# Second-table gathers of 32 slots for four tokens, mixed in TensorE's four column groups

## The chip, the cores and the metric
The kernel runs on one core of one Trainium2 chip. The metric is the device time of one execution in microseconds, lower is better.

## The reference
One inference step of a two-layer trunk for 512 prompt tokens and 8 sample tokens, in float32 with a model width of 1024. Each layer has a mixer (retention in layer 0, an S5 state space in layer 1) and a PEER expert mixer. The change lies in PEER:

```python
def peer_block(xb, w_q, key1, key2, u_tab, v_tab):
    q = (xb @ w_q).reshape(T, PEER_HEADS, 2, PEER_DQ // 2)          # 8 heads
    s1 = einsum('thd,hkd->thk', q[:, :, 0], key1)                    # 128 keys a side
    s2 = einsum('thd,hkd->thk', q[:, :, 1], key2)
    v1, i1 = top_k(s1, 16);  v2, i2 = top_k(s2, 16)
    cand = (v1[..., :, None] + v2[..., None, :]).reshape(T, PEER_HEADS, 256)
    cidx = (i1[..., :, None] * 128 + i2[..., None, :]).reshape(T, PEER_HEADS, 256)
    top, sel = top_k(cand, 16)
    eidx = take_along_axis(cidx, sel, axis=-1)                       # 8 x 16 = 128 experts a token
    gate = softmax(top, axis=-1)
    act = gelu(einsum('thkd,td->thk', take(u_tab, eidx), xb))
    return einsum('thk,thkd->td', gate * act, take(v_tab, eidx))
```

Both tables have 16384 rows of 1024 numbers (4 KB) per layer. For each token 128 rows of `u_tab` are multiplied with the token's vector, and 128 rows of `v_tab` are summed with the weights that result.

## The kernel before
The prompt is four tiles of 128 tokens, one token to a partition; the samples are a fifth tile of 8 rows. A token's 128 experts are its slots. A chunk is 32 slots (two heads) of one tile (`CH`), four chunks make a tile (`PARTS`), 16 a layer (`CHUNKS`).

Pool (GpSimd) issues every table gather by an indirect DMA: row p of the gather is the table row that token p's index names, so one gather brings one slot of 128 tokens, 128 rows of 4 KB. Rows of the first table (u) land in `v_ring` during the first two chunks and in `u_ring` after that, rows of the second (v) in `v_ring`; each has 8 places (`RING`). The order is written out by hand in Pool's `peer`: the first two chunks are u alone, then a u gather of chunk j alternates with a v gather of chunk j-2 (`LAG`). After the last u come v gathers alone, from `LATE` on (the last 16 slots) with the 8 sample gathers ahead of them. A gather waits until its place is free: u places by `u_used` (DVE), v places by `v_used` (PE) or `v_added` (DVE).

DVE multiplies each u row with the token's vector and sums it (L2346). Between these products stand pieces of the selection of the next chunk (`best_of`), the softmax, and the weights of the chunk before. For a v slot ACT writes a 128x128 diagonal of the slot's weights (`diagonal`, L1620), and PE multiplies the diagonal with the 128 gathered rows (`mix`, L1982; two matmuls, which the profile shows as four records), summing in two PSUM banks per tile. Eight diagonals exist (`DIAGS`); ACT waits for PE before it writes one again. 19 slots near the end of a layer (`DVE_SLOTS`) are summed by DVE instead (L2389). The selection of a chunk begins with scores on PE (L1929) and their copy by ACT (`scores_in`, L1591), which stands in ACT's program behind the diagonal of slot 14 of a chunk and waits for `top_done`, a finished selection that frees the buffer. In chunks 7, 9, 11 and 12 two scores are computed, one of them for the samples.

At the end of a layer `sample_mix` (L1967) multiplies the sample rows, and DVE adds each tile's sum to the residual (`mixed`, L2311 and L2315), the last tile's when its last slot is summed; the norm for the next part follows.

## Time and profile before

| | |
|---|---|
| median of 3 runs | 4188.11 us (4186.7 to 4188.8) |
| profiled execution, span from its first to its last instruction | 4188.0 us, mean granted TensorE clock 0.952 |
| PE busy | 3358.3 us (80%) |
| DVE busy | 2484.9 us (59%) |
| Pool busy | 2098.5 us (50%) |
| ACT busy | 690.1 us (16%) |
| DMA | 1293.90 MB, mean 309 GB/s |

Shares of busy time are means over the retention, SSM and PEER parts, which have different limits; a stage is read by its own windows and by what ended the waits in it. In a timeline row the first number is the start, the second the duration, and the bracket is how long the engine was idle just before and who ended that.

### The profile page before, as it was taken

The page shows a single profiled execution, that of the slowest core. Times are in us where ns is not written, and L with a number is a line of the kernel's source. Part 1 is how long each engine was busy: PE and PEld are TensorE (multiplying, and loading weights), DVE is VectorE, ACT ScalarE, POOL GpSimd, SP SyncE. Part 2 cuts the span into 40 slices and gives each one's busy share as a digit, 9 for nine tenths or more (in the row PEclk, how much of TensorE's full clock was granted, in tenths as well). Part 3 has the DMA queues.
Part 4 walks back from the last instruction along what each step waited for, and adds up shares of the span by engine and source line. Part 5 has one row for each costly group of instructions (what it writes and reads, how often), then busy time and mean ns, then how long its engine had stood idle before and what let it go on. Part 6 is the DMA issues. An engine that isn't in the chain of part 4 may idle for free.

```text
span 4188.0 us, 31521 instructions
## 1 busy us (share of the span) xinstructions
PE 3358.3 (80%) x9470; PEld 1378.2 (33%) x9470; DVE 2484.9 (59%) x5918; ACT 690.1 (16%) x1670; POOL 2098.5 (50%) x2213
## 2 busy tenths in 40 slices
PE   6899999996777777777778847996777787768777
PEld 1343443463222222222222334452222232223222
DVE  4334334449666776778652483259667676877643
ACT  2211111111111111111111232101111111111111
POOL 1110010016777767777775010026777677767766
PEclk8799999998999999999999968998999999989999
DMA  9943243249999999999999344159999999999998
GB/s 333 312 151 121 96 145 116 95 143 338 409 409 409 409 392 404 409 402 394 406 409 392 109 44 142 46 185 367 409 409 409 409 394 406 409 399 396 409 409 309
DMA packets 409876, 1293.90 MB, mean 309 GB/s; under 512 B 50094, under 2 KB 73806, under 8 KB 408687
## 3 DMA queue, kind: packets, MB, share of 16 engines
q0 software_dynamic: 309312, 1126.31, 68.6%
q1 hardware_dynamic: 100232, 163.58, 12.3%
q10 hardware_dynamic: 180, 2.18, 0.2%
q8 instruction: 71, 1.16, 0.1%
q14 instruction: 81, 0.66, 0.0%
HBM read 1263.06 MB, written 28.85 MB: 308 GB/s over the span
## 4 chain that ended last, share of the span: by engine, by line
PE 30%; DMA 26%; POOL 20%; DVE 13%; issue 8%; ACT 2%; SPq 1%; DVEq 0%; POOLq 0%; ACTq 0%
DMA arena<-in_peer_v_dram,arena 13%; DMA w<-in_peer_u_dram,arena 11%; POOL arena L1362 10%; POOL w L1362 9%; PE ps L1802 8%; PE ps L1982 5%; DVE arena L2346 3%; PE ps L1894 3%; DVE w L2346 3%; PE ps L809 3%; PE ps L1949 3%; DMA w<-in_w_ada_dram 2%; PE ps L701 1%; PE ps L1760 1%; PE ps L1735 1%
## 5 line engine op out<-in xcount | busy, mean ns | idle before, releaser
L1982 PE MATMUL ps<-arena 128*128 128x512 f32 x3944 | 1946.0, 623 | 642.7 <-DMA arena<-in_peer_v_dram,arena 553.4
L2346 DVE CUSTOM_DVE_ANT_0 w<-w,ps 128x1024 f32<-128x1024 f32 x896 | 1090.1, 1218 | 695.8 <-DMA w<-in_peer_u_dram,arena 694.1
L1982 PEld LDWEIGHTS ps<-arena 128*128 128x128 f32 x3944 | 691.9, 192 | 1872.1 <-DMA arena<-in_peer_v_dram,arena 1220.7
L1362 POOL DMA_INDIRECT arena<-in_peer_v_dram,arena x1040 | 1000.9, 962 | 431.4 <-issue 239.7
L1362 POOL DMA_INDIRECT w<-in_peer_u_dram,arena x912 | 860.6, 944 | 280.8 <-issue 249.4
L1620 ACT ACTIVATE arena<-ident,arena 128x128 f32<-128x128 f32 x986 | 377.2, 398 | 1611.9 <-PE ps L1982 1587.1
L1802 PE MATMUL ps<-w,hT 128*128 128x512 f32 x768 | 341.7, 598 | 0.0
L1949 PE MATMUL ps<-hT,w 128*128 128x512 f32 (+1 forms) x512 | 262.2, 605 | 0.0
L1362 POOL DMA_INDIRECT arena<-in_peer_u_dram,arena x128 | 124.6, 974 | 217.3 <-DVE arena L2346 143.6
L1802 PEld LDWEIGHTS ps<-w,hT 128*128 128x128 f32 x768 | 142.7, 190 | 195.7 <-issue 175.4
L1303 POOL TENSOR_TENSOR rstd<-var,mhalf 128x1 f32<-128x1 f32 x25 | 16.5, 666 | 287.9 <-DVE var L2015 287.9
L2346 DVE CUSTOM_DVE_ANT_0 arena<-arena,ps 128x1024 f32<-128x1024 f32 x128 | 151.8, 1214 | 9.7 <-DMA arena<-in_peer_u_dram,arena 9.7
L1334 POOL DMA_DIRECT2D out_dram<-arena x16 | 11.6, 726 | 281.3 <-DVE arena L2118 276.6
L1894 PE MATMUL ps<-w,arena 128*128 128x512 f32 (+1 forms) x320 | 142.0, 598 | 0.0
L1950 PEld LDWEIGHTS ps<-hT,w 128*128 128x128 f32 x512 | 97.3, 190 | 108.7 <-issue 91.8
L2389 DVE SCALAR_TENSOR_TENSOR arena<-arena 128x1024 f32<-128x1024 f32 x36 | 46.3, 1287 | 114.4 <-DMA arena<-in_peer_v_dram,arena 114.2
L2194 DVE MAX8 arena<-modp 128x8 f32<-128x128 f32 (+1 forms) x160 | 34.6, 277 | 102.4 <-ACT modp L1591 102.4
L1529 ACT ACTIVATE arena<-ps 128x512 f32<-128x512 f32 (+1 forms) x60 | 35.7, 595 | 349.8 <-PE ps L1802 345.2
L1342 POOL TENSOR_TENSOR rstd<-var,mhalf 128x1 f32<-128x1 f32 x20 | 12.8, 640 | 154.5 <-DVE var L2099 154.5
L535 POOL MEMSET arena<- 64x2048 f32 x4 | 10.7, 2672 | 157.1 <-DVEq L1041 157.0
L1296 POOL TENSOR_TENSOR mods<-arena 9x1024 f32<-9x1024 f32 x4 | 11.2, 2799 | 150.2 <-ACT arena L1482 150.2
L2346 DVE DVE_READ_ACCUMULATOR2_ANT arena<- 128x1 f32 x1024 | 84.2, 82 | 0.0
(319 smaller groups left out, 2962.6 us busy)
## 6 DMA issues: line engine op xcount, KB each, us to landing
w<-in_w_ada_dram SPq DMA_DIRECT2D x32, 1024.0 KB, 11.7
w<-in_ret_w_in_dram SPq DMA_DIRECT2D x24, 1024.0 KB, 7.3
arena<-in_peer_v_dram,arena POOLq DMA_INDIRECT x1040, 10.3
x<-in_w_ada_dram SPq DMA_DIRECT2D x16, 1024.0 KB, 11.6
w<-in_peer_w_q_dram SPq DMA_DIRECT2D x16, 1024.0 KB, 8.0
w<-in_peer_u_dram,arena POOLq DMA_INDIRECT x912, 10.8
out_dram<-arena POOLq DMA_DIRECT2D x20, 512.0 KB, 5.0
arena<-in_state_ret_dram POOLq DMA_DIRECT2D x16, 512.0 KB, 6.0
```

The source lines that it names most:

```text
L701: mm = pe.matmul(ps[:, t % 2, :], hT[:, c, t * P:(t + 1) * P], block_rows(b)[:, c, :], start=(c == 0), stop=(c == KC - 1))
L809: mm = pe.matmul(ps[:, 2 * (n % 2) + b, :], hT[:, c, t * P:(t + 1) * P], rows_of[b][:, c, :], start=(c == 0), stop=(c == KC - 1))
L1362: pool.indirect_dma_start(ring[:, slot, :], None, table, bass.IndirectOffsetOnAxis(ap=index, axis=0)).then_inc(landed_sem[slot], 16)
L1620: act.activation(diag[:, n % DIAGS], ident[:, :], ACT.Copy, scale=wgt[:, m % 4, s:s + 1]).then_inc(diag_done, 1)
L1735: mm = pe.matmul(ps[32 * j:32 * j + 32, 1 + n % 2, :], condT[:, c, :], ada_rows[slot][:, c, :], start=(c < 4), stop=(c >= 4))
L1802: mm = pe.matmul(ps[:, bank, :], hT[:, c, t * P:(t + 1) * P], block_rows(j % 2)[:, c, :], start=(c == 0), stop=(c == KC - 1))
L1894: mm = pe.matmul(ps[0:rows, n % 4, :], oT[:, c, t * P:t * P + rows], rows_out[:, c, half * BW:(half + 1) * BW], start=(c == 0), stop=(c == 3))
L1949: pe.matmul(ps[:, n % 2, first:TP * P], wq, hT[:, c, first:TP * P], start=(c == 0), stop=(c == KC - 1))
L1950: mm = pe.matmul(ps[:, 2 + n % 2, 0:NS], wq, hT[:, c, TP * P:NTOK], start=(c == 0), stop=(c == KC - 1))
L1982: mm = pe.matmul(ps[:, bank + half, :], diag[:, n % DIAGS], v_ring[:, n % RING, half * BW:(half + 1) * BW], start=(n % NE == 0), stop=(n % ...
L2346: dve.tensor_tensor_reduce(row, row, h_ps, 1.0, 0.0, ALU.mult, ALU.add, acts[:, j % 2, s:s + 1]).then_inc(u_used, 1)
L2389: dve.scalar_tensor_tensor(v_sum, v_ring[:, n % RING], weight, v_sum, ALU.mult, ALU.add)\
```

## The change
A v gather no longer brings one slot of 128 tokens, but the chunk's 32 slots of four tokens: partition 32q+s holds slot s of token 32j+8q+r, for q = 0 to 3. A chunk has 32 such gathers, numbered 4r+j. The index table for it, `eidx_t`, is made by PE, which turns a chunk's places (`turn_places`: four matmuls against strided columns of the identity), and DVE, which copies them out of PSUM (`places_out`). Four gathers (j = 0 to 3) make a batch. In it column group j of PE (32 columns, so 32 PSUM partitions) multiplies gather j with 32 columns of a zeroed strip (`windows`) in which four columns hold the turned weights, so that each of the four tokens gets the sum over its 32 slots. The strip's place slides with r. The weights are turned by PE (`turn_weights`) and copied into the strip by ACT (`windows_of`), once per chunk and not once per slot. The diagonals and the slots summed by DVE are gone. A batch is 8 matmuls of 32x512 (16 records); its four places come free together. Three semaphores are new (`turned_ps`/`turned_done`, `windows_ps`/`windows_done`, and PE's waits on `score_done` ahead of the turns, which use the scores' banks). `gated`, the product in `mixed`, moves to other memory, and DVE clears `windows` once per layer.

```diff
-DIAGS = 8
+GROUPS = 4
+TURNS_IN = CH // GROUPS
+WINDOWS = TURNS_IN * (NE + 1)
...
-DVE_SLOTS = ([CH * (CHUNKS - 2) + s for s in range(11, CH, 3)] + [CH * (CHUNKS - 1) + s for s in range(2, 15, 3)] +
-             [LATE + s for s in range(0, 13, 2)])
...
+        by_group = ident.rearrange("p (j q r) -> p q r j", j=GROUPS, q=GROUPS)
...
+        turned_places = ps[:, 4, 0:2 * CH]
+        turned_weights = ps[:, 5, 0:CH]
...
                 def v_gather(n):
                     place = v_place(n)
                     if n < RING:
                         pool.wait_ge(u_used, used_before(layer, SWITCH - RING + n + 1))
                     else:
-                        v_free(place - RING)
-                    gather(v_ring, place % RING, vt, eidx[:, n // NE, n % NE:n % NE + 1], v_ld)
+                        pool.wait_ge(v_used, used_before(layer, place - RING + 1))
+                    if n % CH == 0:
+                        pool.wait_ge(turned_done, CHUNKS * layer + n // CH + 1)
+                    gather(v_ring, place % RING, vt, eidx_t[:, n // CH, n % CH:n % CH + 1], v_ld)
...
-                def diagonal(m, s):
-
-                    n = TP * NE * layer + CH * m + s
-                    if CH * m + s in DVE_SLOTS:
-                        return
-                    if s == 0:
-                        act.wait_ge(wgt_done, (CHUNKS + 1) * layer + m + 1)
-                    if CH * m + s >= DIAGS:
-                        act.wait_ge(v_used, mixed_before(layer, v_place(CH * m + s - DIAGS) + 1))
-                    act.activation(diag[:, n % DIAGS], ident[:, :], ACT.Copy, scale=wgt[:, m % 4, s:s + 1]).then_inc(diag_done, 1)
+                def windows_of(m):
+
+                    act.wait_ge(windows_ps, CHUNKS * layer + m + 1)
+                    if m >= 2:
+                        act.wait_ge(v_used, used_before(layer, v_place(CH * (m - 1) - 1) + 1))
+                    rows_of = windows[:, m % 2].rearrange("p (r n) -> p r n", n=NE + 1)
+                    for q in range(GROUPS):
+                        part_ = slice(CH * q, CH * (q + 1))
+                        at = TURNS_IN * q
+                        ins = act.activation(rows_of[part_, :, at:at + 3 * CH + 1:CH],
+                                             turned_weights[part_].rearrange("p (r j) -> p r j", j=GROUPS), ACT.Copy)
+                    ins.then_inc(windows_done, 1)
...
+                windows_of(0)
+                for j in range(LAG, CHUNKS + 1):
+                    tanh_of(j - 1)
+                    if j == CHUNKS:
+                        for i in range(TP - 1):
+                            squares(k, i)
+                        tanh_of(CHUNKS)
+                    if j + 1 < CHUNKS:
+                        for p in TOPS[j + 1]:
+                            scores_in(p)
+                    if j < CHUNKS:
+                        for p in TOPS[j]:
+                            exponentials(p)
+                    windows_of(j - 1)
...
+                def turn(out, source):
+
+                    for q in range(GROUPS):
+                        mm = pe.matmul(out[CH * q:CH * (q + 1)], source, by_group[:, q], start=True, stop=True)
+                    return mm
+
+                def turn_places(m):
+
+                    pe.wait_ge(top_done, picked_at(layer, PLACE[m // PARTS, m % PARTS]))
+                    if m >= 2:
+                        pe.wait_ge(turned_done, CHUNKS * layer + m)
+                    at = CH if m == 1 else 0
+                    turn(turned_places[:, at:at + CH], place[:, m % 3]).then_inc(turned_ps, 1)
+
+                def turn_weights(m):
+
+                    pe.wait_ge(wgt_done, (CHUNKS + 1) * layer + m + 1)
+                    if m:
+                        pe.wait_ge(windows_done, CHUNKS * layer + m)
+                    turn(turned_weights, wgt[:, m % 4]).then_inc(windows_ps, 1)
+
+                def mix(m, r):
+
+                    t, bank = m // PARTS, 2 * (m // PARTS % 2)
+                    if m % PARTS == 0 and r == 0 and t >= 2:
                         pe.wait_ge(mix_free, TILES * layer + t - 1)
-                    pe.wait_ge(v_ld[n % RING], landed(layer, v_place(n)))
-                    pe.wait_ge(diag_done, diagonals_before(layer, n + 1))
+                    if r == 0:
+                        pe.wait_ge(windows_done, CHUNKS * layer + m + 1)
+                    n = CH * m + GROUPS * r
+                    for j in range(GROUPS):
+                        pe.wait_ge(v_ld[(n + j) % RING], landed(layer, v_place(n + j)))
                     for half in range(2):
-                        mm = pe.matmul(ps[:, bank + half, :], diag[:, n % DIAGS],
-                                       v_ring[:, n % RING, half * BW:(half + 1) * BW],
-                                       start=(n % NE == 0), stop=(n % NE == NE - 1))
-                    mm.then_inc(v_used, 1)
-
+                        for j in range(GROUPS):
+                            at = NE * r + CH * j
+                            mm = pe.matmul(ps[CH * j:CH * (j + 1), bank + half, :], windows[:, m % 2, at:at + CH],
+                                           v_ring[:, (n + j) % RING, half * BW:(half + 1) * BW],
+                                           start=(m % PARTS == 0 and r == 0),
+                                           stop=(m % PARTS == PARTS - 1 and r == TURNS_IN - 1))
+                            if half:
+                                mm.then_inc(v_used, 1)
+
+                pe.wait_ge(score_done, picked_at(layer, TOPS[1][-1]))
+                turn_places(0)
+                turn_places(1)
+                pe.wait_ge(score_done, picked_at(layer, TOPS[2][-1]))
+                turn_weights(0)
                 for j in range(LAG, CHUNKS + LAG):
                     tops = TOPS[j + 1] if j + 1 < CHUNKS else []
-                    for s in range(CH):
-                        if CH * (j - LAG) + s == LATE:
+                    if j < CHUNKS:
+                        if TOPS[j]:
+                            pe.wait_ge(score_done, picked_at(layer, TOPS[j][-1]))
+                        turn_places(j)
+                    for r in range(TURNS_IN):
+                        if CH * (j - LAG) + GROUPS * r == LATE:
                             sample_mix()
-                        mix(j - LAG, s)
-                        if s == 8 and tops:
+                        mix(j - LAG, r)
+                        if r == 2 and tops:
+                            pe.wait_ge(turned_done, CHUNKS * layer + j + 1)
                             scores(tops[0])
-                        if s == 12 and len(tops) > 1:
+                        if r == 3 and len(tops) > 1:
                             scores(tops[1])
-                        if s == 8 and j == CHUNKS - 1:
+                        if r == 2 and j == CHUNKS - 1:
 
                             pe.wait_ge(score_done, TURNS * (layer + 1))
                             pe.wait_ge(gate_done, layer + 1)
+                            pe.wait_ge(turned_done, CHUNKS * (layer + 1))
                             pe.transpose(ps[:, 4, 0:NS], place_s[0:NS], ident[0:NS, 0:NS])
                             pe.transpose(ps[:, 4, NS:2 * NS], gate[0:NS, TP], ident[0:NS, 0:NS]).then_inc(es_ps, 1)
+                        if r == TURNS_IN - 2 and j <= CHUNKS:
+                            if tops:
+                                pe.wait_ge(score_done, picked_at(layer, tops[-1]))
+                            turn_weights(j - 1)
...
+                def places_out(m, n):
+                    dve.wait_ge(turned_ps, CHUNKS * layer + m + n)
+                    dve.tensor_copy(eidx_t[:, m:m + n].rearrange("p m n -> p (m n)"), turned_places[:, 0:n * CH])\
+                       .then_inc(turned_done, n)
...
+                        if s == 28 and j == LAG - 1:
+                            places_out(0, 2)
+                        if s == 4 and j >= LAG:
+                            places_out(j, 1)
...
-                for i, n in enumerate(DVE_SLOTS):
-                    if n == CH * (CHUNKS - 1) + 11:
-                        weights_out((CHUNKS + 1) * (layer + 1), acts_s, acts_s2, gate_s, wgt_s[:, ::NS + 1])
-                    weight = wgt[:, n // CH % 4, n % CH:n % CH + 1]
-                    dve.wait_ge(v_ld[n % RING], landed(layer, v_place(n)))
-                    if i == 0:
-                        dve.tensor_scalar(v_sum, v_ring[:, n % RING], weight, None, ALU.mult).then_inc(v_added, 1)
-                    else:
-                        dve.scalar_tensor_tensor(v_sum, v_ring[:, n % RING], weight, v_sum, ALU.mult, ALU.add)\
-                           .then_inc(v_added, 1)
-                    if n == CH * (CHUNKS - 1) + 14:
-                        for i in range(TP - 1):
-                            variance(k, i)
-                    if n >= LATE + 2 and n <= LATE + 6:
-                        normalized(k, (n - LATE - 2) // 2)
-                    dve.wait_ge(v_added, added(layer, n))
-                link.link(dve.tensor_tensor(v_sum, v_sum, modp[:, 2], ALU.mult))
-                dve.wait_ge(v_used, mixed_before(layer, LATE + NS))
+                weights_out((CHUNKS + 1) * (layer + 1), acts_s, acts_s2, gate_s, wgt_s[:, ::NS + 1])
+                for i in range(TP - 1):
+                    variance(k, i)
+                for i in range(TP - 1):
+                    normalized(k, i)
```


PE's program at the first chunks that are mixed, in the kernel before (L1929 scores, L1982 mix):

```order
L1929 MATMUL ps<-arena 128x128 x2
L1982 MATMUL ps<-arena 128x512 x18
L1929 MATMUL ps<-arena 128x128 x4
L1982 MATMUL ps<-arena 128x512 x64
L1929 MATMUL ps<-arena 128x128 x4
L1982 MATMUL ps<-arena 128x512 x64
```

The same place after the change (L1921 scores, L1966 turns, L1997 mix):

```order
L1921 MATMUL ps<-arena 128x128 x2
L1966 MATMUL ps<-ident,arena 32x32 x16
L1997 MATMUL ps<-arena 32x512 x24
L1921 MATMUL ps<-arena 128x128 x4
L1997 MATMUL ps<-arena 32x512 x32
L1966 MATMUL ps<-ident,arena 32x32 x4
L1997 MATMUL ps<-arena 32x512 x8
L1966 MATMUL ps<-ident,arena 32x32 x4
L1997 MATMUL ps<-arena 32x512 x24
```

The scores moved from behind slot 8 to behind the third batch (slots 8 to 11); the turned weights of the next chunk stand behind the seventh batch, and the turned places of a chunk ahead of the first batch of the chunk two before it.

ACT's program around chunk 7 before, with the semaphores that each waits for (L1591 copies of scores, L1620 diagonals, L1609 tanh, L1597 exponentials):

```order
L1620 ACTIVATE arena<-ident,arena 128x128 [waits v_used,wgt_done]
L1620 ACTIVATE arena<-ident,arena 128x128 [waits v_used] x4
L1609 ACTIVATE arena<-arena 128x32 [waits gelu_in]
L1620 ACTIVATE arena<-ident,arena 128x128 [waits v_used] x10
L1591 ACTIVATE modp<-ps 128x512 [waits top_done,score_ps]
L1591 ACTIVATE modp<-ps 8x512 [waits top_done,score_ps]
L1620 ACTIVATE arena<-ident,arena 128x128 [waits v_used] x12
L1597 ACTIVATE arena<-arena 128x32 [waits e_sub]
```

After (L1581 copies of scores, L1599 tanh, L1587 exponentials, L1610 the copies into the strip):

```order
L1599 ACTIVATE arena<-arena 128x32 [waits gelu_in]
L1581 ACTIVATE modp<-ps 128x512 [waits top_done,score_ps]
L1581 ACTIVATE modp<-ps 8x512 [waits top_done,score_ps]
L1587 ACTIVATE arena<-arena 128x32 [waits e_sub]
L1610 ACTIVATE arena<-ps 32x8x4 [waits v_used,windows_ps]
L1610 ACTIVATE arena<-ps 32x8x4 x3
```

Behind the two score copies, which still wait for `top_done`, no work for the running chunk is left; the copies into the strip belong to the next one.

Pool's program where the first v gather of a layer stands, after the change (before, this gather waits for `u_used` alone):

```order
L1357 DMA arena<-in_peer_u_dram,arena 128x1024 [waits u_used] x31
L1357 DMA w<-in_peer_u_dram,arena 128x1024 [waits u_used,q_ps,top_done]
L1357 DMA arena<-in_peer_v_dram,arena 128x1024 [waits turned_done,u_used]
L1357 DMA w<-in_peer_u_dram,arena 128x1024 [waits u_used]
L1357 DMA arena<-in_peer_v_dram,arena 128x1024 [waits u_used]
```

The gather itself stands where it stood; a wait for DVE's copy of the turned places is new in front of it.

## Rows read from the trace of the kernel before

**Rows 1.** The page: two rows of the 40 slices, a fortieth of the span each.

```profile
DMA  9943243249999999999999344159999999999998
GB/s 333 312 151 121 96 145 116 95 143 338 409 409 409 409 392 404 409 402 394 406 409 392 109 44 142 46 185 367 409 409 409 409 394 406 409 399 396 409 409 309
```

**Rows 2.** The page's costliest groups: busy and mean, then idle before and its end.

```profile
L1982 PE MATMUL ps<-arena 128*128 128x512 f32 x3944 | 1946.0, 623 | 642.7 <-DMA arena<-in_peer_v_dram,arena 553.4
...
L1620 ACT ACTIVATE arena<-ident,arena 128x128 f32<-128x128 f32 x986 | 377.2, 398 | 1611.9 <-PE ps L1982 1587.1
```

**Rows 3.** The timeline in the mixed stretch: an issue, and a slot's mix.

```profile
2001.43 0.94 POOL L1362 DMA_INDIRECT w<-in_peer_u_dram,arena  x1 [0.30 <-issue]
...
2003.20 1.98 PE L1982 MATMUL ps<-arena 128*128 128x512 f32 x4 [0.58 <-DMA arena<-in_peer_v_dram,arena]
```

**Rows 4.** Windows: stretch, length, busy times, PEclk, DMA share, GB/s.

```profile
1100.00:1400.00 300.00, 231.92 (x496) 82.04 (x494) 202.60 (x518) 48.74 (x128) 226.27 (x240) 1.00 1.03 409
1440.00:1940.00 500.00, 383.59 (x850) 146.55 (x848) 370.35 (x1023) 80.68 (x220) 355.41 (x376) 0.95 1.01 400
3300.00:3800.00 500.00, 381.93 (x850) 145.38 (x848) 370.39 (x1023) 80.50 (x221) 355.54 (x377) 0.96 1.01 401
```

**Rows 5.** The timeline around one dent of layer 0.

```profile
1488.93 0.59 ACT L1591 ACTIVATE modp<-ps 8x512 f32<-8x512 f32 x1 [23.59 <-DVE arena L2278]
...
1489.96 7.40 PE L1982 MATMUL ps<-arena 128*128 128x512 f32 x12 [9.84 <-ACT arena L1620]
...
1493.98 0.94 POOL L1362 DMA_INDIRECT arena<-in_peer_v_dram,arena  x1 [11.42 <-PE ps L1982]
```

**Rows 6.** The waits: total, times, longest.

```profile
PE ps L1982 <- ACT arena L1620: 85.1, 8, 13.1
```

**Rows 7.** The timeline at the first v gather of layer 0.

```profile
1020.21 0.93 POOL L1362 DMA_INDIRECT arena<-in_peer_v_dram,arena  x1 [0.30 <-issue]
...
1021.51 1.22 DVE L2346 CUSTOM_DVE_ANT_0 arena<-arena,ps 128x1024 f32<-128x1024 f32 x1
...
1026.42 0.21 DVE L2298 TENSOR_SCALAR arena<-arena 128x32 f32<-128x32 f32 x1
...
1026.77 1.22 DVE L2346 CUSTOM_DVE_ANT_0 w<-w,ps 128x1024 f32<-128x1024 f32 x1
```

**Rows 8.** PE's timeline near the start: two groups of 16 records with 32 columns.

```profile
11.14 3.64 PE L1735 MATMUL ps<-w,arena 128*32 128x512 f32 x16 [2.53 <-DMA w<-in_w_ada_dram]
...
113.73 1.92 PE L1735 MATMUL ps<-w,arena 128*32 128x512 f32 x16
```

**Rows 9.** Issue to landing, median, in 985:1000, 1100:1200 and 4100:4126.

```profile
arena<-in_peer_u_dram,arena POOLq DMA_INDIRECT x8, 5.4
...
arena<-in_peer_v_dram,arena POOLq DMA_INDIRECT x40, 10.0
...
arena<-in_peer_v_dram,arena POOLq DMA_INDIRECT x19, 6.3
```

**Rows 10.** Layer 1's tail: first lone v gather, first sample gather, the last tile's sum.

```profile
4081.65 0.94 POOL L1362 DMA_INDIRECT arena<-in_peer_v_dram,arena  x1 [4.70 <-PE ps L1982]
...
4128.73 1.76 POOL L1362 DMA_INDIRECT arena<-in_peer_v_dram,arena  x1 [0.30 <-issue]
...
4176.51 1.22 DVE L2311 TENSOR_TENSOR arena<-ps,modp 128x1024 f32<-128x1024 f32 x1
```

**Rows 11.** Layer 0's tail: the same three, and PE's sample mix.

```profile
2259.53 0.94 POOL L1362 DMA_INDIRECT arena<-in_peer_v_dram,arena  x1 [0.30 <-issue]
...
2277.27 0.94 POOL L1362 DMA_INDIRECT arena<-in_peer_v_dram,arena  x1 [0.30 <-issue]
...
2285.38 13.90 PE L1967 MATMUL ps<-arena 128*8 128x512 f32 x32
...
2320.29 1.22 DVE L2311 TENSOR_TENSOR arena<-ps,modp 128x1024 f32<-128x1024 f32 x1
```

**Rows 12.** PE's timeline in layer 1, where bursts and pauses alternate.

```profile
4070.05 2.81 PE L1982 MATMUL ps<-arena 128*128 128x512 f32 x4 [2.51 <-DMA arena<-in_peer_v_dram,arena]
```

More of the change, by code:

```diff
@@ L249, in build @@
         wgt = cut(4, CH)
-        diag = cut(DIAGS, P)
+        windows = cut(2, WINDOWS)
         best = cut(4, TOPK)
@@ L255, in build @@
         topi = cut(2, TOPK, dtype=U32)
-        place = cut(CH)
+        place = cut(3, CH)
         place_s = cut(NE)
@@ L323, in v_place @@
             return n if n < LATE else n + NS
-        def mixed_before(layer, place):
-            return (SLOTS - len(DVE_SLOTS)) * layer + place - sum(v_place(d) < place for d in DVE_SLOTS)
-        def diagonals_before(layer, n):
-            return (TP * NE - len(DVE_SLOTS)) * layer + n - sum(d < n for d in DVE_SLOTS)
-        def added(layer, n):
-            return len(DVE_SLOTS) * layer + DVE_SLOTS.index(n) + 1
         def landed(layer, n):
@@ L1375, in u_gather @@
                     gather(v_ring if n < SWITCH else u_ring, n % RING, ut, eidx[:, n // NE, n % NE:n % NE + 1], u_ld)
-                def v_free(place):
-                    for n in DVE_SLOTS:
-                        if v_place(n) == place:
-                            pool.wait_ge(v_added, added(layer, n))
-                            return
-                    pool.wait_ge(v_used, mixed_before(layer, place + 1))
                 def v_gather(n):
@@ L1407, in peer @@
                 for b in range(NS):
-                    v_free(LATE + b - RING)
+                    pool.wait_ge(v_used, used_before(layer, LATE + b - RING + 1))
                     gather(v_ring, b, vt, eidx_s[:, b:b + 1], v_ld)
@@ L1987, in peer @@
+                pe.wait_ge(score_done, picked_at(layer, TOPS[1][-1]))
[3 more added lines that the diff above has]
+                turn_weights(0)
                 for j in range(LAG, CHUNKS + LAG):
                     tops = TOPS[j + 1] if j + 1 < CHUNKS else []
-                    for s in range(CH):
-                        if CH * (j - LAG) + s == LATE:
+                    if j < CHUNKS:
[4 more added lines that the diff above has]
+                        if CH * (j - LAG) + GROUPS * r == LATE:
@@ L2276, in best_of @@
                 else:
-                    link.link(dve.tensor_tensor(place[rows], side1[rows], side2[rows], ALU.add))
-                    dve.tensor_copy(eidx[rows, t, c * CH:(c + 1) * CH], place[rows]).then_inc(top_done, 1)
+                    whole = place[rows, (PARTS * t + c) % 3]
+                    link.link(dve.tensor_tensor(whole, side1[rows], side2[rows], ALU.add))
+                    dve.tensor_copy(eidx[rows, t, c * CH:(c + 1) * CH], whole).then_inc(top_done, 1)
                 yield
@@ L2310, in mixed @@
                 mod = (modp if t < TP else mods)[0:rows, 2]
-                link.link(dve.tensor_tensor(gated[0:rows], ps[0:rows, bank:bank + 2, :],
+                product = (gated if t < TP - 1 else gated_last)[0:rows]
+                link.link(dve.tensor_tensor(product, ps[0:rows, bank:bank + 2, :],
                                             mod.rearrange("p (a n) -> p a n", a=2), ALU.mult))
@@ L2314, in mixed @@
                 xt = x[0:rows, t].rearrange("p (a n) -> p a n", a=2)
-                link.link(dve.tensor_tensor(xt, xt, gated[0:rows], ALU.add))
+                link.link(dve.tensor_tensor(xt, xt, product, ALU.add))
                 dve.sem_inc(x_ready, 1)
@@ L2329, in chunk_out @@
                     if j >= 4:
-                        dve.wait_ge(diag_done, diagonals_before(layer, CH * (j - 3)))
+                        dve.wait_ge(windows_ps, CHUNKS * layer + j - 3)
                     link.sync()
```

38 lines of the change are left out of this document (11 added, 27 removed).

## The prediction
> **What bounds the kernel now.** I read the page's slices first. Two long stretches, one per layer's PEER part, stand at 409 GB/s with the DMA row at 9 [rows 1]: the gathers. The page's largest group is PE's mixing of the second table (1946.0 us), but its idle time, 642.7 us, was ended mostly by DMA (553.4) [rows 2]: PE waits for rows, so its busy time is no price. A gather is 128 rows of 4 KB, 0.524 MB, and at 409 GB/s takes 0.524288/0.409 = 1.28 us. Pool needs 0.94 us for an issue and 0.30 to the next, 1.24 in all, and PE spends 1.98 on a second-table slot [rows 3], of which one comes every 2.56 us. So DMA sets the pace (1.28), Pool is 3% under it, PE has a quarter of its time free.
>
> The view by windows then tells where the stream is not full: 1100 to 1400 runs at 409 GB/s, 1440 to 1940 of layer 0 at 400 and 3300 to 3800 of layer 1 at 401, where PE's granted clock is 0.95 and 0.96 [rows 4]. The timeline of one of the dents shows the chain: ACT had waited 23.59 us at the score copy for DVE, the diagonals stood behind it, PE idled 9.84 us for one, and Pool 11.42 us for PE to free a slot [rows 5]. The waits of the whole span list this PE wait 8 times, 85.1 us [rows 6]: four dents per layer, where a chunk scores twice and the second copy needs a finished selection.
>
> **What the change removes.** The diagonals go. ACT's long wait stays, but what is queued behind it now is one copy of turned weights for the next chunk, needed only a quarter of a chunk later; DVE's selection ends near slot 20 of a chunk, PE turns weights behind slot 27. Nothing in the mix waits for ACT inside a chunk. The lost bytes come back: (409-400)/409 x 500 = 11.0 us and (409-401)/409 x 500 = 9.8 us, **-20.8**. The 85.1 us are no price, since Pool's queue of issued gathers covers part of each wait. Bounds: 0 if another wait takes the place, -20.8 as the rate allows no more.
>
> The 986 diagonal copies (377.2 us of ACT) [rows 2] and the slots that DVE sums lie beside DMA-bound work, so they are worth nothing, except in the tails below.
>
> **What it adds at the head.** The first second-table gather was issued at 1020.21, with nothing ahead of it but Pool's own pace. Now it waits for the indices that PE turns and DVE copies out behind DVE's product of slot 60, which starts at 1021.51 and takes 1.22 [rows 7]; a copy of 64 columns is near the 0.21 us that DVE needs for an operation on 32 [rows 7], so with the signal Pool goes on at about 1022.96, 2.75 later. Behind this wait stand all later issues of Pool; DVE's first product on a u_ring row (1026.77) came at once [rows 7], the next ones come late. The queue is shallow there, so I count nearly all, 2.6 in each layer: **+5.2** (bounds 0, were it caught up at 1.24 against 1.28, and 5.5). Later chunks turn their indices at slot 4 of the chunk two ahead of their use: covered by two chunks, some 160 us.
>
> **The mix itself.** A batch is 16 records of 32 columns. The trace has that shape elsewhere: 1.92 us with the four column groups side by side, 3.64 for the same records after an idle PE [rows 8], which is the full and the half clock. The same work took 4 x 1.98 = 7.92. In the mixed stretch a batch is due every 4 x 2.56 = 10.24 us, so either is hidden. What counts there is the release of slots in fours: the first gather that needs a batch's slots is ten issues behind the batch's last, so a cycle of eight gathers needs latency + mix + 0.30 - 2 x 1.24. From issue to landing a gather takes 5.4 us where the queue is short, 10.0 where it is full [rows 9]; the 10.0 contain the queue, which a waiting Pool shortens by itself. With 5.4 and 3.64 the need is 6.86 against 10.24, and it binds only from a latency of 8.78. Cost 0; its bound is rival B.
>
> **The tails.** Behind the last first-table rows Pool issues second-table gathers alone, and eight slots are all there is. Before: 33 gathers between 4081.65 and 4128.73 (1.427 each, 5.71 per four) in layer 1 [rows 10], 13 between 2259.53 and 2277.27 (1.365, 5.46 per four) in layer 0 [rows 11]. Now two batches alternate: 3 x 1.24 for the other issues of a batch, latency 5.4 (6.3 was seen in this tail [rows 9], with a pace of 1.43), mix, 0.30, all halved: 5.67 per batch with a mix of 1.92, 6.53 with 3.64. For the mix I take 3.2: bursts of 1.98 with pauses of 2.51 grew to 2.81 [rows 12], by 1.42, which makes 2.73 of 1.92, and these pauses are longer, so halfway to 3.64. That is 6.31 per batch: 33/4 x 0.60 = +4.9 and 13/4 x 0.85 = +2.8, **+7.7** together; bounds -0.3 and +6.8 in layer 1, +0.7 and +3.5 in layer 0.
>
> The last 24 gathers (8 of samples, 16 of the prompt) gain. Counted from the first sample issue s, the last tile's sum started at s+47.8 in layer 1 (4176.51-4128.73) [rows 10] and s+43.0 in layer 0 (2320.29-2277.27) [rows 11]. Now the sample mix starts at s+5.7 and lasts 13.90 [rows 11], to s+19.6; the eighth prompt gather waits for the slot freed last, lands 5.7 later at s+25.3 and is mixed at s+28.5; the last batch follows after 0.3+3.72+5.4+3.2 at s+41.1. Gains 6.7 and 1.9, **-8.6**; bounds s+38.6 with all mixes at 1.92, s+43.4 with 3.64 and 1.5 more for a sample mix that starts at half clock (the 12 records of 7.40 in [rows 5] instead of 12/4 x 1.98). Tails together -0.9, from -13.2 to +6.3.
>
> Sum: -20.8+5.2-0.9 = -16.5. Ahead of the tails, gathers share DMA with the bulk loads of the next part, and batches there can miss their turn; I put +1 for each layer by choice (0 to 3). So -14.5 from the profiled span of 4188.0, which equals the median of 4188.1: **4174 us**.
>
> **The clock.** PE will often restart from idle. The rows show both levels: 16 records in 1.92 or 3.64 [rows 8]. The Trainium skill, "TensorE: Matmul & The Clock Gate", section on HAM oscillation, says that a loop whose matmul bursts are shorter than its DMA waits restarts at half clock every time. By that rule every batch takes 3.64, the tails come to +6.3, and the time is 4181; by the full-clock row alone it is 4161. The trace agrees half: 1.98 grew to 2.81, not 3.96 [rows 12].
>
> **Rivals.** A: other waits eat the gain, or the tails run cold and the shared stretch costs 3 each. For it: five new waits, a tail that has only two batches in flight. Against it: the order puts each new wait a quarter chunk or more behind its producer. Cold tails, the shared stretch at +3 each and a quarter of the dents left: -20.8+5.2+6.3+6+5.2 = +1.9, 4190; without that quarter 4185.
>
> B, the other side: the ring is too shallow for release in fours. Place: Pool's wait for a used slot in the mixed stretch. If latency stays at the loaded 10.0 whatever Pool does, a cycle takes 10.0+3.64+0.30-2.48 = 11.46, 1.22 over 10.24, 224 times (14 chunks of 8 batches in 2 layers): +273, 4450 us. It decides from a latency of 8.78; 0.06 beyond it uses up the gain. For it: the 10.0 of [rows 9]. Against it: 5.4 at a short queue. That the column groups do not run side by side would do the same: 5.4+7.92+0.30-2.48 = 11.14, +202; [rows 8] speak against it.
>
> C: the rows of a gather now belong to four tokens, each with 16 picks of two heads that share key halves, and experts of one second key lie multiples of 512 KB apart. If this slows reading, each per cent of 1.28 us over 1040 gathers is 13.3 us; about 1.1% decides, 3% gives 4214. No row of before has such addresses. The Trainium skill, "DMA: Bandwidth & Descriptors", section on latency and other measured facts, lists copies with a row pitch of 512 KiB at 207 GB/s and of 4 MiB at 103, against 214 with a padded pitch; no run shown here has such a pitch, and the picks of a head are mixed, not one pitch.
>
> D: PE at full clock everywhere and the head half caught up: -20.8+2.6-13.2 = 4157.
>
> **Chances.** Forecast 0.62 (0.50 faster, 0.12 within), A 0.18 (0.15 within, 0.03 slower), B 0.09, C 0.07 (0.02 within, 0.05 slower), D 0.04 (faster). What a measurement of this kernel can tell from no change is about 0.2%, 8.4 us. So faster 0.54, same 0.29, slower 0.17. For the range, B and most of C (0.14) are left out above, and a little of D below: 4158 to 4198.
>
> **What would show it.** Right: 408 GB/s or more over 1440 to 1940, no PE wait for ACT there, Pool idle for PE below 0.4 us per eight gathers; the first second-table gather some 1.45 us behind the start of DVE's slot-60 product; batches of 1.9 to 3.7 us; in the tail four gathers per 5.7 to 6.5 us. Wrong: regular Pool waits of over 1 us in the mixed stretch (B), a rate below 409 with a full queue (C), a PE wait at the first batch of a chunk (A), batches near 8 us.

## The result: slower, and the profile after

The changed kernel takes 4224.4 us (median of 4 runs, 4220.66 to 4229.48) where the kernel before takes 4188.12: 1.0086 times as long, interval 1.0074 to 1.0098. The forecast of 4174 was wrong, in sign too. The profiled execution spans 4224.2 us.

The page of after, slices and the groups that answer to [rows 1] and [rows 2] (ACT's copies into the strip stand where the diagonals stood):

```profile
PEclk8799999997556566565566868996665655665557
GB/s 334 305 146 124 97 142 123 88 151 332 409 409 409 407 405 405 405 405 405 401 405 333 110 43 141 46 204 356 409 409 406 406 404 406 404 405 402 409 376 279
...
L1997 PE MATMUL ps<-arena 128*32 128x512 f32 x4096 | 907.6, 1034 | 1638.2 <-DMA arena<-in_peer_v_dram,arena 1638.2
...
L1610 ACT ACTIVATE arena<-ps 32x32 f32<-32x32 f32 x128 | 27.8, 217 | 1128.2 <-PE ps L1966 1127.1
```

The windows of after, for [rows 4]:

```profile
1440.00:1940.00 500.00, 185.77 (x944) 48.96 (x944) 371.41 (x1031) 15.87 (x51) 366.54 (x386) 0.60 1.02 405
3300.00:3800.00 500.00, 189.04 (x956) 50.64 (x960) 371.14 (x1031) 15.87 (x51) 369.47 (x386) 0.62 1.02 405
```

The deep dents (the eight stretches in which PE waited for a diagonal) are gone and PE never waits for ACT in the mix, as forecast; the rate is 405 GB/s, not the 408 that the forecast asked for. The 256 batches take 907.6 us, 3.55 each and 200 of them over 3.5, near the 3.64 of the half clock [rows 8]. Yet nothing was won. To find where the time is, I set marks in DVE's timeline: the start of the first product on a u_ring row, of the product 32 slots later, of the last sample's product, and of the last tile's sum. The marks of after:

```profile
1031.13 1.21 DVE L2386 CUSTOM_DVE_ANT_0 w<-w,ps 128x1024 f32<-128x1024 f32 x1
...
1116.16 1.22 DVE L2386 CUSTOM_DVE_ANT_0 w<-w,ps 128x1024 f32<-128x1024 f32 x1 [0.56 <-DMA w<-in_peer_u_dram,arena]
...
2225.28 1.23 DVE L2418 CUSTOM_DVE_ANT_0 w<-w,arena 128x1024 f32<-128x1024 f32 x1 [1.47 <-DMA arena<-hs_d]
...
2341.60 1.23 DVE L2345 TENSOR_TENSOR arena<-ps,modp 128x1024 f32<-128x1024 f32 x1 [20.50 <-PE ps L1997]
...
4097.95 1.22 DVE L2418 CUSTOM_DVE_ANT_0 w<-w,arena 128x1024 f32<-128x1024 f32 x1 [1.31 <-DMA arena<-hs_d]
...
4212.76 1.22 DVE L2345 TENSOR_TENSOR arena<-ps,modp 128x1024 f32<-128x1024 f32 x1 [23.46 <-PE ps L1997]
```

Before, the product 32 slots in (layer 0) and the last sample products:

```profile
1108.27 1.22 DVE L2346 CUSTOM_DVE_ANT_0 w<-w,ps 128x1024 f32<-128x1024 f32 x1 [0.65 <-DMA w<-in_peer_u_dram,arena]
...
2220.45 1.23 DVE L2374 CUSTOM_DVE_ANT_0 w<-w,arena 128x1024 f32<-128x1024 f32 x1 [1.33 <-DMA arena<-hs_d]
...
4077.47 1.22 DVE L2374 CUSTOM_DVE_ANT_0 w<-w,arena 128x1024 f32<-128x1024 f32 x1 [1.33 <-DMA arena<-hs_d]
```

With the other marks of before in [rows 7, 10, 11] and the same rows of layer 1, the 36.2 us by which the profiled span grew divide so:

| stretch | layer 0: before, after | layer 1: before, after | difference | forecast |
|---|---|---|---|---|
| up to the first u_ring product | 1026.77, 1031.13 | | +4.4 | 0 |
| next 32 products (head) | 81.50, 85.03 | 81.49, 84.61 | +3.5, +3.1 | +5.2 |
| to the last sample product (mixed) | 1112.18, 1109.12 | 1108.94, 1107.67 | -3.1, -1.3 | -20.8 |
| to the last tile's sum (tail) | 99.84, 116.32 | 99.04, 114.81 | +16.5, +15.8 | -0.9+2 |
| from there to layer 1's first u_ring product | 566.75, 564.07 | | -2.7 | 0 |

The first 4.4 arise ahead of all changed work, around the first loads; in the profiles of the variants below the same mark lies 0.4 to 6.3 us behind that of before, with no order that follows the edits, so I take it for spread between executions; no run shows what makes it.

The tails carry the loss. Timeline of after in layer 1's tail, Pool and PE:

```profile
4117.40 0.94 POOL L1357 DMA_INDIRECT arena<-in_peer_v_dram,arena  x1 [5.21 <-issue]
...
4121.14 0.94 POOL L1357 DMA_INDIRECT arena<-in_peer_v_dram,arena  x1 [0.30 <-issue]
...
4127.28 3.29 PE L1997 MATMUL ps<-arena 128*32 128x512 f32 x16 [8.00 <-DMA arena<-in_peer_v_dram,arena]
...
4130.82 0.94 POOL L1357 DMA_INDIRECT arena<-in_peer_v_dram,arena  x1 [3.76 <-PE ps L1997]
...
4132.59 2.80 PE L1997 MATMUL ps<-arena 128*32 128x512 f32 x16 [2.02 <-DMA arena<-in_peer_v_dram,arena]
...
4141.16 3.64 PE L1997 MATMUL ps<-arena 128*32 128x512 f32 x16 [5.66 <-DMA arena<-in_peer_v_dram,arena]
...
4145.02 0.94 POOL L1357 DMA_INDIRECT arena<-in_peer_v_dram,arena  x1 [4.57 <-PE ps L1997]
```

Pool issues eight gathers from 4117.40 on, then has no place. The fourth, issued at 4121.14, lands 6.14 later, the batch takes 3.29, and 0.25 later Pool goes on: eight gathers in 13.4 us here and in 14.2 the next time, 6.9 per four where before took 5.71 [rows 10], and where the forecast's sign of being right was 5.7 to 6.5.

### The profile page after: what moved, and what is told of

Its sections match the earlier page's. It is cut to its first block, busy times and chain, and to the rows that moved or that the text cites. A ratio compares the mean times of both kernels' runs of the same rounds, so it can differ in the third digit from the quotient of the medians.

```text
span 4224.2 us, 31589 instructions
## 1 busy us (share of the span) xinstructions
PE 2351.4 (56%) x10134; PEld 896.1 (21%) x10134; DVE 2440.7 (58%) x5908; ACT 348.2 (8%) x812; POOL 2098.4 (50%) x2213
## 4 chain that ended last, share of the span: by engine, by line
DMA 34%; PE 29%; DVE 14%; POOL 14%; issue 6%; ACT 2%; SPq 1%; POOLq 0%; DVEq 0%; ACTq 0%
DMA w<-in_peer_u_dram,arena 20%; DMA arena<-in_peer_v_dram,arena 11%; PE ps L1794 8%; POOL arena L1357 7%; POOL w L1357 6%; DVE w L2386 5%; PE ps L1997 4%; PE ps L1886 3%; DVE arena L2386 3%; PE ps L804 3%; PE ps L1941 3%; DMA w<-in_w_ada_dram 2%; PE ps L696 1%; PE ps L1752 1%; PE ps L1727 1%
## 5 line engine op out<-in xcount | busy, mean ns | idle before, releaser
L1997 PE MATMUL ps<-arena 128*32 128x512 f32 x4096 | 907.6, 1034 | 1638.2 <-DMA arena<-in_peer_v_dram,arena 1638.2
L1357 POOL DMA_INDIRECT arena<-in_peer_v_dram,arena x1040 | 985.8, 948 | 473.7 <-issue 264.3
L1357 POOL DMA_INDIRECT w<-in_peer_u_dram,arena x912 | 876.4, 961 | 278.1 <-issue 168.5
L1997 PEld LDWEIGHTS ps<-arena 128*32 128x32 f32 x4096 | 173.1, 157 | 2234.7 <-issue 2234.7
L1329 POOL DMA_DIRECT2D out_dram<-arena x16 | 11.6, 727 | 280.3 <-DVE arena L2150 280.3
L1610 ACT ACTIVATE arena<-ps 32x32 f32<-32x32 f32 x128 | 27.8, 217 | 1128.2 <-PE ps L1966 1127.1
L1942 PEld LDWEIGHTS ps<-hT,w 128*128 128x128 f32 x512 | 97.3, 190 | 108.7 <-issue 91.8
L1581 ACT ACTIVATE modp<-ps 128x512 f32<-128x512 f32 (+1 forms) x40 | 23.8, 595 | 966.5 <-PE ps L1921 855.4
L1941 PEld LDWEIGHTS ps<-hT,w 128*128 128x128 f32 x512 | 77.7, 192 | 0.0
## 6 DMA issues: line engine op xcount, KB each, us to landing
x<-in_w_ada_dram SPq DMA_DIRECT2D x16, 1024.0 KB, 11.6
```

The source lines that it names most:

```text
L1357: pool.indirect_dma_start(ring[:, slot, :], None, table, bass.IndirectOffsetOnAxis(ap=index, axis=0)).then_inc(landed_sem[slot], 16)
L1941: pe.matmul(ps[:, n % 2, first:TP * P], wq, hT[:, c, first:TP * P], start=(c == 0), stop=(c == KC - 1))
L1942: mm = pe.matmul(ps[:, 2 + n % 2, 0:NS], wq, hT[:, c, TP * P:NTOK], start=(c == 0), stop=(c == KC - 1))
L1997: mm = pe.matmul(ps[CH * j:CH * (j + 1), bank + half, :], windows[:, m % 2, at:at + CH], v_ring[:, (n + j) % RING, half * BW:(half + 1) * BW],
```

## The experiments

Theory 1: eight places released in fours leave Pool too short a lead. Rival 2: rows of four tokens are read more slowly. Rival 3: PE's half clock. The first four runs are to tell these apart. Pool's lead is how far its issues run ahead of the landings; it is read as the time from a gather's issue to its landing.

**pairs.** A batch in two steps (the loop over `first` and its waits are new):

```diff
-                    for j in range(GROUPS):
-                        pe.wait_ge(v_ld[(n + j) % RING], landed(layer, v_place(n + j)))
+                    step = 2
+                    for first in range(0, GROUPS, step):
+                        for j in range(first, first + step):
+                            pe.wait_ge(v_ld[(n + j) % RING], landed(layer, v_place(n + j)))
...
-                        for j in range(GROUPS):
+                            for j in range(first, first + step):
```

> The change as it is, but a batch of four gathers is mixed in two steps of two: PE waits for two gathers, multiplies them in two column groups, and frees their two places. The rows that a gather brings stay those of four tokens. Theory 1 (release in fours keeps Pool's lead short): a place comes free in time for a latency of 14 issues x 1.28 - 2.0 - 0.3 = 15.6 us instead of 10 x 1.28 - 3.64 - 0.3 = 8.9, so the median from issue to landing late in the mixed stretch rises from 9.0 to about 15, Pool's lead of 11.7 us per layer at the end of the mixed stretch is mostly back, the dents stay away, and Pool alone (1.24) paces the tail: about 4170, between 4160 and 4185. Rival 2 (the rows of four tokens are read more slowly): the rows are the same, so 4224 within 6. Rival 3 (half clock of PE): bursts of 2 us every 5 us instead of 3.6 every 10; only the tail gains, about 4215.

4185.57 us (4181.27 to 4187.73), 0.999 of before (0.998 to 0.9999): 39 us less than the change. The expected 4170 was missed, and its range of 4160 to 4185 by a little; the tails fell to 97.95 and 91.20 us, the mixed stretch stayed (1109.59 and 1108.18).

**singles_mixed.** `step = 1 if m < CHUNKS - LAG else GROUPS`.

> The change as it is, but in the 14 chunks whose gathers alternate with first-table gathers each gather is mixed by itself as it lands (one column group, its place freed at once); the last two chunks stay in batches of four. Theory 1: the latency may grow to 16 x 1.28 - 2.3 = 18.2 us, the lead at the end of the mixed stretch is that of before (11.7 us per layer back), the small dents go: 23 from the lead and up to 15 from the dents, 4186 to 4200. What stays is the tail in fours. Rival 2 (rows of four tokens): 4224 within 6. Rival 3 (half clock): PE is busy 2 us in 2.56 again and stays at the full clock in the mixed stretch, which also lifts the limit of the latency a little, by 1.7 us; 4220.

4229.92 us (4229.42 to 4233.38). This struck theory 1 as first put: the lead came back, the time did not. Time from issue to landing, median in 3150 to 3250, of before, after, pairs and this run:

```profile
arena<-in_peer_v_dram,arena POOLq DMA_INDIRECT x40, 17.9
...
arena<-in_peer_v_dram,arena POOLq DMA_INDIRECT x39, 8.8
...
arena<-in_peer_v_dram,arena POOLq DMA_INDIRECT x39, 13.9
...
arena<-in_peer_v_dram,arena POOLq DMA_INDIRECT x41, 16.4
```

The last three lie at or below the bounds that the expectations worked out from the release (8.9, 15.6, 18.2). But the mixed stretch takes 1111.04 us in both layers with the long lead and 1109.12 and 1107.67 with the short one. A lead is only of use where something eats it. The same pair of runs settles rival 3 there: PE's granted clock from 1440 to 1940 is 1.00 in this run and 0.60 in after, so in the mixed stretch the lower clock cost nothing.

**old_rows.** `vt, eidx[...]` in place of `vt, eidx_t[...]` in `v_gather`.

> The change as it is, but the second-table gathers take their indices from the table of before (one slot of 128 tokens), so that the addresses are those of before and all else, waits and batches included, is that of the change; the sums are over other rows than the reference's. Theory 1: nothing moves, 4224 within 6, latency near 9.0. Rival 2 (addresses): the time falls by what the pattern costs; were it the cause, to about 4190.

4226.14 us (4224.06 to 4227.66), tails 117.3 and 114.9: the addresses cost nothing that these runs can tell. Rival 2 falls, and with it the forecast's rival C.

**before_fours.** The kernel before:

```diff
 def v_free(place):
-    for n in DVE_SLOTS:
-        if v_place(n) == place:
-            pool.wait_ge(v_added, added(layer, n))
-            return
-    pool.wait_ge(v_used, mixed_before(layer, place + 1))
+    for p in range(place // 4 * 4, place // 4 * 4 + 4):
+        by_dve = [n for n in DVE_SLOTS if v_place(n) == p]
+        if by_dve:
+            pool.wait_ge(v_added, added(layer, by_dve[0]))
+        else:
+            pool.wait_ge(v_used, mixed_before(layer, p + 1))
```

> The kernel before, with one edit: Pool waits for all four places of an aligned group of four instead of the one it needs; diagonals, rows and the slots summed by DVE stay. Theory 1: the latency is held at 10 x 1.28 - 2.0 - 0.3 = 10.5 us, the lead at the end of the mixed stretch is short by about 9 to 11 us per layer, the dents cost more since less lead covers them, and the tail waits in fours: 4215 to 4235. Rivals 2 and 3 (rows, clock): rows and PE's work are those of before, so 4188 within 4.

4280.01 us (4278.68 to 4283.02), 1.0218, more than expected. Its tails are 115.9 and 114.6, those of the change, with the old rows, full-width matmuls, the slots summed by DVE and a granted clock of 0.94 in the tail: the release in fours alone makes a tail of that length, without the low clock. The windows of layer 1's tail, of after and of this run:

```profile
4098.00:4213.00 115.00, 61.47 (x280) 12.97 (x280) 8.92 (x19) 2.22 (x7) 60.60 (x64) 0.70 0.82 294
...
4151.00:4266.00 115.00, 89.76 (x184) 31.80 (x182) 35.31 (x40) 16.33 (x41) 65.01 (x64) 0.94 0.84 293
```

Its mixed stretch grew by 28 and 31 us per layer, though PE's waits for ACT are those of [rows 6]:

```profile
PE ps L1983 <- ACT arena L1621: 85.5, 8, 14.1
```

Its lead, in the same view as above:

```profile
arena<-in_peer_v_dram,arena POOLq DMA_INDIRECT x38, 10.0
```

So one and the same wait of PE costs 7 to 8 us each here and next to nothing in before. Ahead of the four dents of layer 0 the lead was 18.3, 12.4, 12.4 and about 10 us in before and 8.5 to 10.8 here, and Pool's longest wait for a place was 11.4 us there and 14.0 here, where it waits for four. How much of the cost is the shorter lead and how much the longer wait no run parts.

**pairs_tail.** `step = GROUPS if m < CHUNKS - LAG else 2`.

> The change as it is, in fours in the 14 chunks that alternate with first-table gathers, and in two steps of two gathers in the last two chunks alone. Theory 1a (the loss sits where second-table gathers are alone, since there eight places are all the queue there is): the time from the last first-table product to the last tile's sum falls from 116.3 and 114.8 us to that of the pairs everywhere (98.0 and 91.2), the mixed stretch stays at the change's pace, 4186 within 5. Theory 1b (Pool's lead out of the mixed stretch is what the tail lives on): the lead is still short at the start of the tail, so about half comes back: 4200 to 4212.

4181.46 us (4178.77 to 4186.14), 0.9987 (0.9978 to 0.9997): all of the loss comes back with the last two chunks alone, tails 98.6 and 89.7. Theory 1a. Layer 1's tail is 9.3 us shorter than that of before: its 33 gathers ahead of the samples take 42.25 us, 1.28 each, where before took 47.08. The granted clock came back with the smaller steps:

```profile
4078.00:4168.00 90.00, 70.03 (x272) 16.86 (x272) 8.99 (x19) 2.22 (x7) 57.88 (x62) 0.97 0.95 375
```

So this run alone does not part the release from the clock; before_fours does. The slots summed by DVE are gone here too, so their removal is not the loss.

**pairs_early.** `if s == 20 and j == LAG - 1` ahead of `places_out(0, 2)`, with pairs everywhere.

> Pairs everywhere, and DVE copies the first turned indices out behind slot 20 of chunk 1 and not behind slot 28; PE had them turned 26 us earlier. If the head's wait costs what it did in the trace of the change (3.7 us in layer 0, 3.0 in layer 1): 4185.6 - 6.7 = 4179 within 4. If Pool's pause there is filled later: 4185 within 3.

4179.28 us (4176.47 to 4183.74), 0.9979 (0.997 to 0.9989): 6.3 less than pairs, as expected. Against the kernel before run beside each it is 0.11%, 4.6 us, and the two intervals overlap; the trace shows it directly, for the head's 32 products take 81.80 and 80.99 us again, where pairs took 84.60 and 84.79.

**before_late_copy.** The kernel before:

```diff
 if s == 14:
-    for p in tops:
+    for p in tops[:1]:
         scores_in(p)
+if s == 26:
+    for p in tops[1:]:
+        scores_in(p)
```

> The kernel before, with one edit: in the four chunks with two scores, ACT copies the second score behind the diagonal of slot 25 and not of slot 14, where DVE's selection is done; so ACT holds no diagonal back, and the dents go. By the forecast's reading (the rate by windows, 400 and 401 against 409) the time falls by 20.8 us, to 4169. By the pace at which first-table rows land (32 slots every 82.75 us, and only 1.4 to 3.1 us more per layer in the chunks with dents), it falls by 2 to 5, to 4185 within 3.

4188.45 us (4181.45 to 4194.43), 1.0000 (0.999 to 1.001). Its windows:

```profile
1440.00:1940.00 500.00, 389.45 (x851) 138.62 (x849) 370.69 (x1023) 82.63 (x219) 366.67 (x384) 1.00 1.02 407
3300.00:3800.00 500.00, 389.04 (x851) 138.56 (x849) 370.66 (x1025) 82.60 (x219) 367.06 (x384) 1.00 1.02 408
```

The dents are gone, the rate is up by 7 GB/s, PE's clock is 1.00, and the mixed stretch takes 1111.74 and 1108.51 us where before took 1112.18 and 1108.94.

**fours_warm, fours_warm2.** Fillers ahead of each batch of the change, four and six:

```diff
+if m >= CHUNKS - LAG:
+    for _ in range(4 if r % 2 else 1):
+        pe.matmul(ps[:, 0, :], ident[:, :], windows[:, m % 2, 0:BW], start=True, stop=True)
 for j in range(GROUPS):
     pe.wait_ge(v_ld[(n + j) % RING], landed(layer, v_place(n + j)))
```

> The change as it is, with filler matmuls on PE in the last two chunks, ahead of each batch (four of 512 columns where the pause is long, one where it is short), into a bank that nobody reads; they only keep PE busy. If half clock is a good part of the tail's cost: batches of 1.92 and not 3.3 to 3.6, per batch (3.72+6.2+1.92+0.3)/2 = 6.1 and not 7.0, so 4226 - 10 in the regular tails - 3 to 6 in the ends: 4210 to 4216. If the release in fours alone makes the tail (the latency of the last of four behind a stalled Pool): 4226 within 4.

4224.07 us (4218.47 to 4229.67). PE still paused ahead of the batch that matters, which took 3.3 us.

> The fillers again, six ahead of the batch behind the long pause, since with four PE still paused for 2.7 to 3.0 us and that batch, which frees the places that Pool waits for, took 3.3 us. If half clock matters: the long-pause batch falls to 1.92 to 2.2, a cycle of eight gathers from 13.7 to 12.3: 8 or 9 us less in the regular tails and 2 to 4 in the ends, 4212 to 4216. If it does not: 4225 within 4.

4224.89 us (4222.21 to 4226.08). Now that batch is short, in the timeline of a cycle:

```profile
4117.85 0.94 POOL L1357 DMA_INDIRECT arena<-in_peer_v_dram,arena  x1 [3.79 <-issue]
...
4121.51 5.42 PE L1994 MATMUL ps<-arena,ident 128*128 128x512 f32 x12
...
4127.73 1.92 PE L2000 MATMUL ps<-arena 128*32 128x512 f32 x16 [0.80 <-DMA arena<-in_peer_v_dram,arena]
...
4129.88 0.94 POOL L1357 DMA_INDIRECT arena<-in_peer_v_dram,arena  x1 [2.39 <-PE ps L2000]
```

That cycle takes 12.0 us, the next two 14.2 and 12.1, where after took 13.6 on average (4117.40 to 4171.80). Layer 1's tail fell by 3.2 to 111.6, layer 0's grew by 1.7 to 118.1; in both, some batches now start right behind fillers, so the fillers stand in the way too. These two runs therefore don't show what half clock costs in the tail, only that fillers don't bring it back. By the forecast's cycle, as an estimate, batches of 1.92 instead of 3.5 would save 0.79 per four gathers, 6.5 of the 11.6 us that layer 1's 33 gathers lost and 2.6 of layer 0's 5.7; a PE at full clock without fillers was not tried with batches of four.

**singles_tail.** `step = GROUPS if m < CHUNKS - LAG else 1`.

> Batches of four in the 14 alternating chunks, and each gather mixed by itself in the last two chunks (one column group, place freed at once). Theory (two limits in the tail: how early places come free, and PE's time per gather): PE needs 1.98 us per gather against 0.96 in pairs and Pool's 1.24, so PE paces the 56 gathers without a first-table partner: about 40 x (1.98 - 1.35) = 25 us per layer in the worst case, less where DMA is shared with bulk loads: 4200 to 4225. Rival (only the release counts): as with pairs, 4181 within 5.

4181.66 us (4176.91 to 4185.83), 0.9981 (0.9972 to 0.999), as with pairs; PE does not pace it. Its timeline shows why:

```profile
4107.73 22.75 PE L1999 MATMUL ps<-arena 128*32 128x512 f32 x71
```

71 records in 22.75 us are 1.28 us per gather of four records, and 1.28 us is the pace at which the gathers land there: PE keeps up, where at the 1.98 that I took from full width it could not. Gathers that follow each other use different column groups, and overlap though each is waited for by itself.

**tail_early.** Pairs in the last two chunks and the early copy of the indices.

> The two edits that helped, together: batches of four in the 14 alternating chunks, two steps of two gathers in the last two chunks, and the first turned indices copied out behind slot 20. If the head's 3.3 us per layer and the tail's cost are independent: 4181.5 - 6.5 = 4175 within 4, faster than both kernels. If what the head gives is taken back by the shared stretch ahead of the tail: 4180 within 3.

4178.2 us (4173.9 to 4182.42), 0.9974 (0.9965 to 0.9983) of before, with medians 11.4 us apart: faster than both kernels. Against the kernel before run beside each, the early copy adds 0.13% (0.9987 to 0.9974), 5.4 us, to what the pairs in the tail give, of the 6.5 expected.

## Why the prediction was wrong

**The dents (-20.8; measured -3.1 and -1.3).** The step "The lost bytes come back" failed. It turned GB/s of a window into time. Without the dents, and with all else as before, the time is the same (before_late_copy). The rows that DVE waits for came nearly on time: two products 32 slots apart lie 82.8 us apart (1274.37 to 1357.20 in before), which is 64 gathers at 405 GB/s, and the mixed stretch holds that pace within 3 us, whether its windows say 400, 405 or 408. Before, a gather landed as late as 17.9 us behind its issue, so far had Pool run ahead, and a wait of 11.42 us [rows 5] was paid out of that; with a release in fours, which shortens the lead and lengthens Pool's wait, the same waits of PE did cost, 28 and 31 us (before_fours). The forecast said itself that the queue covers part; it covered nearly all. Why the windows show 409 where rows are consumed at 405 no run settles.

**The tails (-0.9, plus 2 chosen; measured +32.3).** Three terms were too small. First, in the regular part the mechanism was as described: the cycle is (3.72 + latency + mix + 0.30)/2 as written, but with a latency of 5.7 to 6.6 and a mix of 3.3 to 3.6, not 5.4 and 3.2, 6.8 per four on average and not 6.31: the 33 gathers took +11.6 where I had +4.9 (58.65 from the same gather to the first sample, against 47.08), the 13 of layer 0 +5.7 where I had +2.8. The 6.3 stood in [rows 9] and I took the lower figure; with it the same formula gives +8.7 and +4.2. The Trainium skill, "TensorE: Matmul & The Clock Gate", section on HAM oscillation, has a loop whose matmul bursts are shorter than its DMA waits restart at half clock every time. The trace nearly agrees: 3.55 us per batch, against 3.64. In the mixed stretch that cost nothing; in the tails its share stays open. Second, the end: -6.7 and -1.9 forecast for layers 1 and 0, +0.4 and +3.6 measured. I let the eighth prompt gather go at s+19.6, when its place is free; Pool issued it at s+24.4:

```profile
4176.48 2.39 POOL L1298 TENSOR_TENSOR rstd<-var,mhalf 128x1 f32<-128x1 f32 x3
4179.05 1.49 POOL L1357 DMA_INDIRECT arena<-in_peer_v_dram,arena  x1 [0.18 <-issue]
...
4189.01 0.94 POOL L1357 DMA_INDIRECT arena<-in_peer_v_dram,arena  x1 [0.30 <-issue]
...
4191.80 3.46 PE L1997 MATMUL ps<-arena 128*32 128x512 f32 x16 [6.53 <-DMA arena<-in_peer_v_dram,arena]
...
4195.50 0.94 POOL L1357 DMA_INDIRECT arena<-in_peer_v_dram,arena  x1 [5.55 <-PE ps L1997]
```

Here s is 4164.60. Fifteen issues at 1.24 alone make s+18.6; a wait of 2.5 us for a batch between the fourth and fifth sample gather, Pool's own work (2.39) and two longer issues make the rest. And the path was another than mine: the end hangs not on the eighth prompt gather but on the fourth. The batch that it completes starts at 4191.80, 8.5 us after its issue, the ninth gather waits 5.55 us for the places of that batch, and eight issues in a row, a landing and a last mix of 1.92 follow. Third, the stretch shared with bulk loads, +2 by choice, took +7.2 in layer 0 and +3.8 in layer 1; in layer 0 DMA moved 403 GB/s there before (2220 to 2260) and 353 after (2225 to 2272). That choice stood for more than I saw: [rows 10, 11] call 4081.65 and 2259.53 the first lone v gathers, but Pool's last first-table gathers are issued at 4050.54 and 2193.50, and 8 and 28 lone v gathers stand ahead of those rows. The cycle was priced for 46 of 82.

**The head (+5.2; measured +6.6)** had the right mechanism, and pairs_early shows it by itself; the size lies above its bound of 5.5. I put the signal from DVE to Pool at next to nothing. DVE's copy ends at 1027.13 and Pool goes on 0.77 later:

```profile
1026.91 0.22 DVE L2371 CAST arena<-ps 128x64 uint32<-128x64 f32 x1
...
1027.90 0.94 POOL L1357 DMA_INDIRECT arena<-in_peer_v_dram,arena  x1 [3.75 <-DVE arena L2371]
```

**The rivals.** B had the mechanism, release in fours, and the wrong place. In the mixed stretch the latency settles at 8.8, next to the 8.78 at which I let B begin, and no time is lost; the price is paid where no first-table gathers fill the queue. A had the tails' sign, but allowed 12.3 for them (+6.3 and 3 for each shared stretch) where they took +32.3, and PE's waits ahead of its batches were for rows alone. C is refuted by old_rows. D fell with the 3.55 us of the mean batch.

What the removal of the diagonals is worth shows only against before_fours: with a release in fours the dents would cost some 30 us per layer, and the change avoids that.

## What to carry to other kernels

Price a wait by what it delays at the consumer, not by the bytes missing in a window: the same eight waits of PE cost nothing that these runs can tell where places came free one by one and Pool's lead was 10 to 18 us, and 60 us where they came free in fours and the lead was 8.5 to 10.8. Where places are released in groups, look for the stretch in which that ring is the whole queue, and make the groups small there: two of eight instead of four gave 39 to 43 us. Take the latency from the stretch that is costed, not from the lightest one.

## What the runs showed of the hardware

Matmuls of 32 columns into different column groups overlap also when each waits for its own gather: at most 0.32 us per record of 512 columns in singles_tail, where the landings set the pace, against 0.50 at full width [rows 3]. Gathers of four tokens' 32 picks land as fast as those of 128 tokens' one (4224.4 and 4226.14 us, 8.8 us from issue to landing in both). The batch that takes 1.92 us at a granted clock of 1.00 (4117.36 in after) takes 3.64 at 0.50 (4141.16). The pause ahead of a batch does not tell alone which it will be: in fours_warm three batches took 3.30 to 3.34 us after pauses of 2.7 to 3.0 us; in fours_warm2 one took 1.92 after 0.80, and after the same 2.25 us one took 1.92 (4119.65) and one 3.53 (4132.95).
